# Cache batches in the weights' ring of stage buffers, the latents' copy a batch later, and the prompt's probabilities scaled on GpSimd

## The reference, cut to what matters

```python
# layer B, two groups of tokens
# prompt: 512 new tokens, keys = the prompt's own; sample: 8 streams x 16 tokens,
# keys = 512 cached rows of the stream (cache_ckv, cache_krope) + its 16 new ones
q = rope_part(rmsnorm(x_lat, q_norm) @ w_uq)          # 8 heads x (128 + 64)
k = concat(ckv @ w_uk, krope); v = ckv @ w_uv
p = softmax(mask(q @ k.T * (128 + 64) ** -0.5))
y = x + rmsnorm((p @ v * silu(gate)) @ w_out, norm_post)
```

## Time and profile before

| | |
|---|---|
| median of 3 runs | 804.48 us (803.47 to 805.79) |
| the profiled execution: its own time | 800.87 us |
| its span in the profile | 799.1 us |
| TensorE busy (matmul / weight load) | 83% / 78% |
| VectorE, ScalarE, GpSimd busy | 53%, 37%, 22% |
| mean granted TensorE clock | 0.919 of full speed |

### The profile page before, as it was taken

The page is one execution under the profiler, slowest core; times in us unless marked ns, Lnnn a source line. Parts: engine busy times, 40 slices in busy tenths (PEclk is TensorE's granted clock), DMA queues, the critical chain, the costliest instruction groups (busy, mean ns, idle before and its releaser), DMA issues.

```text
span 799.1 us, 12235 instructions
## 1 busy us (share of the span) xinstructions
PE 660.6 (83%) x4778; PEld 626.4 (78%) x4778; DVE 423.7 (53%) x632; ACT 291.7 (37%) x550; POOL 178.7 (22%) x171
## 2 busy tenths in 40 slices
PE   2797879999999799988979999999974355556996
PEld 2667869999999699978969999899863244446995
DVE  4334347566676763366593575778873222223234
ACT  5263323242332343353242244555554222223221
POOL 4401007025061232154252011000002322221003
PEclk9988899999999899999989999999998676778999
DMA  9201325127142441331341122110443222102303
GB/s 303 66 0 54 106 60 158 54 61 211 57 137 78 141 156 55 93 132 53 94 121 53 53 73 67 48 54 27 121 123 99 66 66 66 66 26 60 153 1 132
DMA packets 66666, 70.83 MB, mean 89 GB/s; under 512 B 9121, under 2 KB 60577, under 8 KB 66482
## 3 DMA queue, kind: packets, MB, share of 16 engines
q1 hardware_dynamic: 66610, 70.06, 28.2%
HBM read 59.27 MB, written 10.78 MB: 88 GB/s over the span
## 4 chain that ended last, share of the span: by engine, by line
PE 69%; DVE 11%; ACT 8%; POOL 5%; DMA 4%; issue 3%; SPq 0%; DVEq 0%; ACTq 0%; POOLq 0%
PE bank L1343 21%; PE bank L1344 20%; PE bank L1345 20%; DMA craw<-in_cache_ckv_dram 3%; DVE slab_lo L1056 3%; POOL skL L823 2%; POOL cn_lo L819 1%; ACT cn_hi L842 1%; PE bank L1385 1%; ACT slab_hi L842 1%; DVE hat_lo L1056 1%; DVE rows L1256 1%; PE bank L1522 1%; POOL stat L777 1%; PE bank L1569 1%
## 5 line engine op out<-in xcount | busy, mean ns | idle before, releaser
L1343 PE MATMUL bank<-slab_hi,hat_hi 128*128 128x256 f32 (+1 forms) x600 | 174.4, 291 | 10.8 <-DVE hat_lo L1056 5.7
L1344 PE MATMUL bank<-slab_lo,hat_hi 128*128 128x256 f32 (+1 forms) x600 | 172.5, 288 | 0.0
L1345 PE MATMUL bank<-slab_hi,hat_lo 128*128 128x256 f32 (+1 forms) x600 | 172.3, 287 | 0.0
L1343 PEld LDWEIGHTS bank<-slab_hi,hat_hi 128*128 128x128 f32 x600 | 118.7, 198 | 12.9 <-DVE hat_lo L1056 6.1
L1345 PEld LDWEIGHTS bank<-slab_hi,hat_lo 128*128 128x128 f32 x600 | 119.3, 199 | 0.0
L1344 PEld LDWEIGHTS bank<-slab_lo,hat_hi 128*128 128x128 f32 x600 | 118.9, 198 | 0.0
L1056 DVE TENSOR_TENSOR slab_lo<-stage,slab_hi 128x1024 fp32r<-128x1024 f32 (+3 forms) x69 | 86.0, 1246 | 12.7 <-ACT slab_hi L842 10.4
L1343 PE MATMUL bank<-hat_hi,slab_hi 128*128 128x320 f32 (+1 forms) x272 | 85.8, 315 | 0.1
L1344 PE MATMUL bank<-hat_lo,slab_hi 128*128 128x320 f32 (+1 forms) x272 | 84.9, 312 | 0.0
L1345 PE MATMUL bank<-hat_hi,slab_lo 128*128 128x320 f32 (+1 forms) x272 | 84.7, 311 | 0.0
L842 ACT ACTIVATE slab_hi<-stage 128x1024 fp32r<-128x1024 f32 (+3 forms) x69 | 70.7, 1025 | 28.9 <-issue 14.5
(11 more groups left out here) (312 smaller groups left out, 1551.8 us busy)
## 6 DMA issues: line engine op xcount, KB each, us to landing
stage<-in_a_w_in_dram SPq DMA_DIRECT2D x24, 512.0 KB, 4.6
stage<-in_b_w_in_dram SPq DMA_DIRECT2D x10, 512.0 KB, 4.1
st_s<-in_state_gla_dram SPq DMA_DIRECT2D x4, 1024.0 KB, 6.6
out_dram<-st_s SPq DMA_DIRECT2D x4, 1024.0 KB, 5.2
stage<-in_a_w_out_dram SPq DMA_DIRECT2D x8, 512.0 KB, 4.5
stage<-in_b_w_out_dram SPq DMA_DIRECT2D x8, 512.0 KB, 3.9
sT_raw<-in_ckvT_dram SPq DMA_DIRECT2D x8, 512.0 KB, 3.7
craw<-in_cache_ckv_dram SPq DMA_DIRECT2D x8, 512.0 KB, 3.9
```

Source lines behind the costliest of these rows:

```text
L1343: pe.matmul(out, a[0], b[0], start=first, stop=False)
L1344: pe.matmul(out, a[0], b[1], start=False, stop=False)
L1345: return pe.matmul(out, a[1], b[0], start=False, stop=last)
```

## The change

1. The raw cache of a sample batch no longer lands where its low half is made. `ct`, `cr` and `cs` become users of the weights' ring of 4 stage buffers (`STAGED` numbers pieces and cache loads together; `load_stage` loads item n + 4 once item n has been consumed), and `ldT`, `ldR`, `ldN` with their semaphores go. What used to hold the load back now holds back ScalarE's copy, which waits for TensorE's last reader of the target. The rotary keys come doubled from DRAM, in one DMA in place of two.
2. `("cs", b + 1)` is done in slot b, where `("cs", b + 2)` was, and stands before `cx`. `ct`, `cr`, `cs` of batches 0 and 1 are spread over heads 4 to 6 and slot 0; `("ss", 0)` moves to the end of head 6, `("ss", 1)` ahead of `O` of head 7; the pieces of a head, of `("wo", "B", 0)` and of `uv` stand behind `qabs`, and `uv` is a head earlier. The early tiles of the output projection, `("y0", 0)` and `("y0", 1)`, move from slots 1 and 3 to slots 5 and 6.
3. `N` keeps only its reciprocal on VectorE; its four multiplications go to GpSimd, and `T` waits for GpSimd. The factor 0.5 goes into the values (`vh`), SCALE into the query latents' norm (`qs`, one more small GpSimd instruction), and the maximum comes negated out of the reduction, so that the two multiplications by -SCALE of a head and the one of a batch go.
4. In the latent part `("gb", 3, 1)` stands behind `("cT", 1)` in place of `("cT", 4)`.

```diff
-    out += [("gb", 3, 0)] + [("cT", t) for t in range(NT)] + [("gb", 3, 1)]
+    out += [("gb", 3, 0), ("cT", 0), ("cT", 1), ("gb", 3, 1), ("cT", 2), ("cT", 3), ("cT", 4)]
...
             out += [("T", h, 0), ("T", h, 1)]
         if h + 1 < HB:
             out += [("S", h + 1, 0), ("S", h + 1, 1), ("N", h + 1, 0), ("N", h + 1, 1)]
+        else:
+            out += [("ss", 1)]
         if h + 2 < HB:
             out += [("qn", h + 2), ("kh", h + 2)]
-        if h >= 0 and h + 4 < HB:
-            load(("hd", h + 4))
-        if h == 4:
-            load(("wo", "B", 0))
-        if h == HB - 2:
-            out += [("ct", 0), ("cr", 0), ("ldR", 1), ("ldN", 1)]
-            load("uv")
-        if h == HB - 1:
-            out += [("ct", 1), ("cr", 1), ("ss", 1), ("ldT", 3), ("ldR", 3)]
         if h >= 0:
             out += [("O", h), ("Oh", h)]
         if h + 2 < HB:
             out += [("qabs", h + 2)]
-        if h == 4:
-            out += [("ldT", 0), ("ldR", 0), ("ldN", 0)]
-        if h == HB - 3:
-            out += [("ldT", 1)]
-        if h == HB - 2:
-            out += [("ss", 0), ("ldT", 2), ("ldR", 2), ("cs", 0)]
+        if 0 <= h < 4:
+            load(("hd", h + 4))
+        elif h == 4:
+            load(("wo", "B", 0))
+            out += [("ct", 0)]
+        elif h == 5:
+            out += [("cr", 0), ("cs", 0)]
+            load("uv")
+        elif h == 6:
+            out += [("ct", 1), ("cr", 1), ("ss", 0)]
...
-    out += [("cs", 1)]
     for b in range(SB):
         out += [("st", b)]
         if b + 2 < SB:
             out += [("ct", b + 2), ("cr", b + 2), ("ss", b + 2)]
-            if b + 4 < SB:
-                out += [("ldT", b + 4), ("ldR", b + 4)]
-        if b in (1, 3):
-            out += [("y0", b // 2)]
+        if b + 1 < SB:
+            out += [("cs", b + 1)]
         if b:
             out += [("cx", b - 1)]
+        if b in (5, 6):
+            out += [("y0", b - 5)]
         if b == SB - 1:
             load(("wo", "B", 1))
             out += [("y0", 2)]
         out += [("sv", b)]
-        if b + 2 < SB:
-            out += [("ldN", b + 2), ("cs", b + 2)]
     out += [("ldk",), ("y0", 3), ("cx", SB - 1)]
 
 
 
 PARTS = {
     "const": ("act",), "piece": ("sp", "pool", "act", "dve"), "lds": ("sp",), "sts": ("sp",), "stp": ("sp",), "ldr": ("sp",),
-    "och": ("sp",), "ldT": ("sp",), "ldR": ("sp",), "ldN": ("sp",), "y0": ("pe", "act", "dve"), "oy": ("sp",), "keep": ("sp",), "ldk": ("sp",), "yt": ("pe", "act"), "xn": ("act", "pool", "dve"), "xT": ("pe", "act", "dve"), "glr": ("pe", "act"),
+    "och": ("sp",), "y0": ("pe", "act", "dve"), "oy": ("sp",), "keep": ("sp",), "ldk": ("sp",), "yt": ("pe", "act"), "xn": ("act", "pool", "dve"), "xT": ("pe", "act", "dve"), "glr": ("pe", "act"),
     "z": ("pe", "dve", "act"), "ln": ("act",), "lg": ("dve",), "lgh": ("act", "dve"), "qp": ("pe",), "rs": ("act",), "c": ("pe", "act"), "e": ("act",),
     "q": ("dve", "act"), "k": ("pe", "dve", "act"), "qlo": ("dve",), "klo": ("dve",),
...
+STAGED = [s for s in STEPS if s[0] in ("piece", "ct", "cr", "cs")]
+STAGED_NO = {s: n for n, s in enumerate(STAGED)}
+assert [s[1:] for s in STAGED if s[0] == "piece"] == [(name, j) for name, pieces in SLABS.items() for j in range(len(pieces))]
+
+
+def stage_counts():
+
+    count, out = [0] * NSTAGE, []
+    for n, step in enumerate(STAGED):
+        windows = SLABS[step[1]][step[2]] if step[0] == "piece" else [("cache", 0, 1)]
+        for w, k0, k1, *_ in windows:
+            count[n % NSTAGE] += 16 * (k1 - k0 if w == "uq_rope" else 1)
+        out.append(count[n % NSTAGE])
+    return out
+
+
+STAGE_COUNT = stage_counts()
...
-        sk_raw = [put(sk_at[i] + 4 * PAST, f"sk_raw{i}", [P, PAST]) for i in range(2)]
-        sT_hi = [put(block_at[(5, 2)[i]], f"sT_hi{i}", [P, KC, PAST], fp32r) for i in range(2)]
-        sT_lo = [put(block_at[(4, 1)[i]], f"sT_lo{i}", [P, KC, PAST], fp32r) for i in range(2)]
-        sT_raw = [put(block_at[(4, 1)[i]], f"sT_raw{i}", [P, KC, PAST]) for i in range(2)]
+        sT_hi = [put(block_at[(5, 1)[i]], f"sT_hi{i}", [P, KC, PAST], fp32r) for i in range(2)]
+        sT_lo = [put(block_at[(4, 2)[i]], f"sT_lo{i}", [P, KC, PAST], fp32r) for i in range(2)]
         cn_hi = [put(block_at[(7, 3)[i]], f"cn_hi{i}", [P, PAST // P, KL], fp32r) for i in range(2)]
         cn_lo = [put((block_at[6], kN_at)[i], f"cn_lo{i}", [P, PAST // P, KL], fp32r) for i in range(2)]
-        craw = [put((block_at[6], kN_at)[i], f"craw{i}", [P, PAST // P, KL]) for i in range(2)]
...
+        def staged_as(kind, step):
+
+            x = stage[STAGED_NO[step] % NSTAGE]
+            if kind == "cr":
+                return x[:, 0:PAST]
+            return x[:, :].rearrange("p (k n) -> p k n", n=PAST if kind == "ct" else KL)
+
...
+            def load_stage(n):
+                step = STAGED[n]
                 if n >= NSTAGE:
-                    after(sp, "dve", "piece", *PIECES[n - NSTAGE])
+                    old = STAGED[n - NSTAGE]
+                    after(sp, parts(old)[-1], *old)
+                if step[0] != "piece":
+                    b, m = step[1], PAST if step[0] == "cr" else KC * PAST
+                    source = {"ct": "ckvT", "cr": "kropeT", "cs": "cache_ckv"}[step[0]]
+                    from_ = dram[source][b]
+                    if step[0] == "ct":
+                        from_ = from_.rearrange("p k n -> p (k n)")
+                    to = stage[n % NSTAGE][:, 0:m]
+                    if step[0] == "cs":
+                        from_, to = from_.rearrange("(s p) n -> p s n", p=P), to.rearrange("p (s n) -> p s n", n=KL)
+                    sp.dma_start(to, from_).then_inc(stage_in[n % NSTAGE], 16)
+                    return
...
+                if step in STAGED_NO:
+                    n = STAGED_NO[step] + NSTAGE
+                    if n < len(STAGED):
+                        load_stage(n)
...
-                elif kind == "ldT":
-                    b = step[1]
-                    after(sp, "pe", *(("ss", b - 2) if b > 1 else ("O", (4, 5)[b])))
-                    sp.dma_start(sT_raw[b % 2][:, :, :], dram["ckvT"][b]).then_inc(turned_in[b % 2], 16)
-                elif kind == "ldR":
-                    b = step[1]
-                    after(sp, "pe", *(("ss", b - 2) if b > 1 else ("S", HB - 1, 1) if b else ("O", 4)))
-                    if b == 1:
-                        after(sp, "pe", "qabs", HB - 1)
-                    for i in range(2):
-                        sp.dma_start(sk_raw[b % 2][i * ROPE:(i + 1) * ROPE, :], dram["kropeT"][b]).then_inc(rotary_in[b % 2], 16)
-                elif kind == "ldN":
-                    b = step[1]
-                    after(sp, "pe", *(("sv", b - 2) if b > 1 else ("S", HB - 1, 1) if b else ("O", 4)))
-                    sp.dma_start(craw[b % 2][:, :, :], dram["cache_ckv"][b].rearrange("(s p) n -> p s n", p=P)).then_inc(cache_in[b % 2], 16)
...
-                    b = step[1]
-                    last = pool.tensor_tensor(cn_lo[b % 2][:, :, :], craw[b % 2][:, :, :], raw(cn_hi[b % 2][:, :, :]), SUB)
+                    b = step[1] % 2
+                    last = pool.tensor_tensor(cn_lo[b][:, :, :], staged_as(kind, step), raw(cn_hi[b][:, :, :]), SUB)
                 elif kind == "cr":
                     after(pool, "act", *step)
-                    b = step[1]
-                    last = pool.tensor_tensor(skL[b % 2][:, :], sk_raw[b % 2][:, :], raw(skS[b % 2][:, :]), SUB)
+                    b = step[1] % 2
+                    last = pool.tensor_tensor(skL[b][:, :], staged_as(kind, step), raw(skS[b][:, :]), SUB)
...
-                    last = pool.tensor_tensor(r, r, minus_half[:, 0:NT], ALU.pow)
+                    link(pool.tensor_tensor(r, r, minus_half[:, 0:NT], ALU.pow))
+                    last = pool.tensor_scalar(r, r, SCALE, None, MUL)
+                elif kind == "N":
+                    after(pool, "dve", *step)
+                    _, h, u = step
+                    for j, (i, c0) in enumerate(zip(UNITS[u], (0, UNITS[u][0] + 1))):
+                        v = prob[u][:, c0:c0 + i + 1, :]
+                        last = pool.tensor_scalar(v, v, S1(("S", h, u), stat2, j), None, MUL)
...
-                    last = copy(values_to(g, 0, t), bank[:, 0, :].rearrange("p (h n) -> p h n", n=VB))
+                    last = act.activation(values_to(g, 0, t), bank[:, 0, :].rearrange("p (h n) -> p h n", n=VB), ACT.Copy, scale=0.5)
...
-                                              ACT.Exp, scale=SCALE, bias=S1(("S", h, u), stat2, j), accum_out=S1(("S", h, u), t=j))
+                                              ACT.Exp, bias=S1(("S", h, u), stat2, j), accum_out=S1(("S", h, u), t=j))
...
-                    b = step[1]
-                    act.wait_ge(turned_in[b % 2], 16 * (b // 2 + 1))
-                    if b == 1:
-
-                        after(act, "pe", "O", 6)
-                    last = copy(sT_hi[b % 2][:, :, :], sT_raw[b % 2][:, :, :])
```

(41 more changed lines are left out.)

53 lines of the change are left out of this document (21 added, 32 removed), and 2 rows, old and new, of the table PARTS.

## The result

The changed kernel takes 771.62 us (median; 767.88 to 773.01) against 803.98 us (802.53 to 805.79) in the same comparison: ratio 0.959, 95% interval 0.955 to 0.963. Forecast were 759 us and a range of 748 to 775. The time lies in the range, but the gain is 32 us where 46 were summed, and it is above the 753 to 766 us that the prediction gave its own sum. Between the two profiles it is 28.7 us (span 799.1 to 770.4), and that is what can be taken apart. The profiled execution of the kernel before was 3.1 us quicker than its median here, the one of the changed kernel 0.6 slower.

The account below looks back on a forecast made before the run. TensorE was taken to bound the heads and a chain of waits the sample loop. Terms -7.9 - 1.3 - 10.0 - 25.8 - 1.3 = -46.3 from 804.48 gave 758, stated as 759 us, range 748 to 775.

Parts of the forecast that it names:

- main term: Sample loop: with the load off the chain, five slots take 65 us for 90.8, -25.8 (-29 to -22).
- signs that it named for being wrong: T waiting for GpSimd, a landing ahead of `ct`, or T or O of head 6 much later than 593 less the shift.
- What bounds the kernel: TensorE bounds heads, 49.9 of 57.9 us busy in projection; sample loop is a chain of waits, 18.2 us a slot.
- The latent part: Before the fourth `cT`: `gb` 3, 1 fills TensorE's 5.71 us wait at full clock, -7.9 (-5.7 to -8.5).
- The sample slot: From one start of `ss` to the next: 13.0 us, ends 12.3 and 13.8, for 18.2 before.
- The clock: Sample slots: stays low in the sum, so `ss` matmuls come at the 1.2 GHz level after a 5.2 us wait.
- The rival of a high clock: Sample slots: clock stays high, 11 us a slot, 10 less, 749 us; 12%.
- The heads: Prompt's heads: TensorE's waits on VectorE go, GpSimd's scaling hidden at 3.4 us a head; -1.3.
- The way in: Last heads into the sample loop, up to `ss` 2: 612.3 for 622.35, -10.0 (-6 to -12).
- The way out: From `ss` 7 to `so`: 26.8 us for 28.1, -1.3.
- the dearer way in: Rival: heads 5 to 7, with ScalarE and VectorE full, give only -4; 765 us, 12%.
- GpSimd's in a mild form: Rival: GpSimd becomes the heads' bound at 5.2 us a head, +9, 768 us; 15%.

Follow-up runs that it names:

- Experiment 2: Kernel before with only the sample loop's order changed: `cs` of batch b+1 in slot b ahead of `cx`, loads and buffers unchanged; 777.25 us, ratio 0.966.
- 11: Kernel before with only the latent part's and the sample loop's order changed, no ring, GpSimd scaling or folded factors; 771.17 us, ratio 0.961.
- experiment 1: Kernel before with only the latent part's order changed: `gb` 3, 1 behind the second `cT` instead of the fifth; 795.02 us, ratio 0.988.
- experiment 8: Changed kernel with twenty idle 512-column matmuls ahead of each score step of batches 2 to 7; 753.53 us, ratio 0.938.
- 9: Changed kernel with `ct` and `cr` of batch b+3 put ahead of the exponential of batch b+2, under its scores; 724.47 us, ratio 0.904.
- Experiment 3: Changed kernel with the four scaling multiplications of a head back on VectorE, folded factors kept; 766.26 us, ratio 0.952.
- Experiment 7: Changed kernel with the copies around heads 4 to 6 directly behind the transposed probabilities and the `uv` pieces not before slot 6; 768.63 us, ratio 0.956.
- experiment 6: Changed kernel with six idle 512-column matmuls in TensorE's 1.47 us wait ahead of `so`; 764.61 us, ratio 0.952.

## Why the prediction was right, and where its sum was not

The mechanism of the main term was right, and the time lies in the range. It is in the range by the room that was left for rivals, though: a sum of -46.3 with ends of 753 to 766 us does not hold 771.6, and the largest single miss, the clock in the projection, stood neither in the sum nor among the rivals. Two of the signs that it named for being wrong came: T waits for GpSimd, and O of head 6 starts at 592.0, where 593 less the shift would be 585.1 (2.0 of the difference are drift).

**What bounds the kernel** was right: the loop was a chain, and the order made it. `cn` was on the chain by its place in two queues alone. But I credited the removal to the ring ("the next load is held by nothing on this chain"). Experiment 2 shows that the place of `cs` takes the landing off the chain by itself, and 11 that the rest of the change adds nothing net. The loop's stretch has TensorE busy for 59% (47.42 of 79.87 us), as forecast.

**The latent part**, -7.9: shown. -7.8 in the profile after and in that of experiment 1, whose medians give -9.6 with an interval of 5.7 us across.

**The sample slot**, 13.0: measured 13.64 in the slot shown. The terms of ScalarE, the maximum and the exponential are right within 0.1. Two were mis-sized: `ss` to the maximum took 5.60 for 5.0, and `skL` 1.86 for 1.65. I had taken 1.65 for `skL` undisturbed, but it runs beside VectorE's `sT_lo` in all of these slots (below). -22.1 in place of -25.8, inside the ends given.

**The clock** was rightly kept low in the sum; that it is the wait that holds it low is shown by experiments 8 and 9. The rival of a high clock was priced at 11 us a slot, which experiment 8 has (11.0), and that is 13.5 us in the five slots, since the measured slot was 13.7.

**The heads**, -1.3 with GpSimd's scaling hidden at 3.4 us a head: the step that failed in kind. The line through two-input products gave 3.4, `skL`'s rate 5.2; measured are 4.4, which end behind the 4.3 us window, so five T steps wait for it (0.35 to 1.02 us). +1.3 in the stretch instead of -1.3, and +0.4 ahead of T of head 0, where most of the -1.3 was to come from. Experiment 3 takes 3.4 us back, 2.4 of them shown by the profiles.

**The way in**, -10.0: -5.8, just outside its own end of -6. Some 1.6 us of this miss lie in the profile of the kernel before: against the way in of experiments 1, 2 and 11 (53.3 to 53.5 us) it is -7.4. The step that failed is O of head 6 "at about 593 instead of 588.4": it was to start 22.4 us behind T of head 5 and started 25.5 behind it. I had named the copies that stand ahead of the transposes' copies, but not their whole effect. T of head 6 came 1.4 us later than in the sum: VectorE's halves of the `wo` pieces and of `ct` 0 stand ahead of `pT_lo` as well, so that in place of the wait of 1.51 us, which was to go and went, TensorE has one of 1.96 us for `pT_lo` (573.35), and behind it the granted clock was 0.50 from 574 to 576. In experiment 3 the wait for `pT_lo` was 2.75 us, the clock stayed at 1.00, and T of head 6 came 14.4 us behind T of head 5 in place of 15.0. Then VectorE's two `uv` halves took 3.95 us for 2.48, because `cn_lo` of GpSimd ran beside them. The last 1.2 us fell between O of head 6 and `ss` 2. Experiment 7 confirms the place: with these copies elsewhere the stretch is 38.6 us.

The row of the `uv` halves (585.49 and 586.25 in experiment 7) is where the rule of the Trainium skill stood ("SBUF — State Buffer", "Who interferes with whom"): of the 1.62 us in which the two overlapped, VectorE lost 1.47, and `cn_lo`, which came first, kept its 2.38. By the rule, the later one is fully blocked, and this row agrees with it. The 0.42 of the earlier trace rows that I went by was no weaker block but a shorter overlap: the `sT_lo` of that slot in the kernel before started 0.58 us before `cn_lo` ended at 710.66. And the 1.65 that I took for `skL` undisturbed was a stretched one. The first line is of the kernel before, the second of the changed kernel, where VectorE stood idle beside it:

```profile
710.08 1.65 DVE L1056 TENSOR_TENSOR sT_lo<-sT_raw,sT_hi 128x1024 fp32r<-128x1024 f32 x1 [0.27 <-ACT sT_hi L842]
```

```profile
584.12 1.30 POOL L818 TENSOR_TENSOR skL<-stage,skS 128x512 fp32r<-128x512 f32 x1 [3.00 <-ACT skS L844]
```

Beside a `sT_lo` that had started first, `skL` took 1.65, 1.86 and 2.07 us with overlaps of 0.53, 0.74 and 0.95 us.

**The way out**, -1.3: -1.36. **Not in the sum**: the projection, +4.7 (experiment 6), and the drift before the heads, +2.0 in the pair of profiles.

With these the difference between sum and profile closes: 46.3 less 3.7 (slots), 4.2 (way in), 2.6 (heads), 0.4 (ahead of T of head 0), 4.7 (projection) and 2.0 (drift) is 28.7, which is what was measured. Of the rivals, the dearer way in (priced at -4) happened in part, and GpSimd's in a mild form.

## What to carry to other kernels

Where engines run their queues in order, ask of each instruction on the chain whether it is there for its data or for its place: two moved entries alone gave as much as this whole change (771.2 us for 771.6), and a third move, copies under the scores of the batch before, was worth more than all of it. Before building a deeper buffer, move the consumer a step later with the buffers as they are, and see whether the wait is still there. Price a short TensorE wait at the clock that follows it as well, and cover it with the next step's work, or with idle matmuls where there is none.

## What the runs showed of the hardware

A wait of 1.47 us was followed by 10 us of matmuls at the 1.2 GHz level, 4.7 us lost, though TensorE had been busy for nearly all of the 20 us before it, at the 2.4 GHz level (the changed kernel's window ahead of that wait, below); with six matmuls in the wait the level held. The length of a wait alone does not tell: between T of head 5 and T of head 6, 1.96 us was followed by about 3 us at the 1.2 GHz level in both profiles of the changed kernel, while 1.51 us (the kernel before) and 2.75 us (experiment 3) were not.

```profile
686.50:706.30 19.80, 19.05 (x160) 18.44 (x159) 9.41 (x17) 9.19 (x18) 4.78 (x2) 1.00 0.36 109
```

GpSimd's tensor_scalar with a factor per partition took 604 ns for 128 elements and 1566 ns for 512, about 0.28 us and 2.5 ns an element, where VectorE took 487 ns for 512.

Where a VectorE subtraction with both inputs in SBUF and one of GpSimd overlapped, the one that started later was longer by nearly the whole overlap, and the first one was not: `slab_lo` by 1.47 us of 1.62, `sT_lo` by 0.42 of 0.58, `skL` by 0.35, 0.56 and 0.77 of 0.53, 0.74 and 0.95. `cn_lo` kept its 2.35 to 2.38 us beside `pT_lo` and `spT_lo`, which take one input from PSUM, and these kept theirs.
